# A slot directive at the head of TensorE's HGRN loop

## The chip, the cores and the metric

The program runs on one core of a Trainium2 chip. The metric is the device time of one execution in microseconds (us), the median of several runs. Each engine of the core (TensorE, VectorE, ScalarE, GpSimd, SyncE) has its own instruction stream and its own sequencer, which reads that stream in order; the engines wait for each other on semaphores only. In the profile TensorE's matmuls are PE, its weight loads PEld, and what its sequencer handles by itself (register, semaphore and branch instructions) PEldq.

## What is computed

Two blocks of network layers over a sequence of 512 tokens and 16 meta tokens, width 1024, in float32. The stage that the change touches is the second layer of the first block, a gated linear recurrence (HGRN2):

```python
def hgrn2_mixer(h, w_in, lb, o_norm, w_out):
    q, fp, i_in, gate = jnp.split(h @ w_in, 4, axis=-1)
    q = jax.nn.silu(q)
    f = lb32 + (1.0 - lb32) * jax.nn.sigmoid(fp32)
    k = (1.0 - lb32) * jax.nn.sigmoid(-fp32)
    ...
    _, o = lax.scan(_hgrn_chunk_step, S0, xs)   # S_t = diag(f_t) S_{t-1} + k_t i_t^T, o_t = S_t^T q_t
    ...
    return (o * jax.nn.silu(gate)) @ w_out
```

There are 16 heads of 128 channels. Ahead of this stage comes a pooling layer, behind it two layers of windowed attention with a gated MLP. All large products are made in three parts: each float32 operand is split into a high and a low part, and high by high, low by high and high by low are accumulated.

## The kernel before

The engines' programs are written out by hand; the order of TensorE's work is the order of the Python code, unrolled, save for one loop. `products` (L402 to L404) issues the three matmuls of one 128x128 tile of weights; `unit` runs it over a whole projection of 128 output channels (24 matmuls of 512 columns, or 48 of 264). Each matmul is two instructions in TensorE's stream, a weight load and the matmul.

The HGRN stage works on pairs of heads, eight in all. `b_pair` (from L1235) makes the eight projections of one pair of heads and, in between, at the places in `STEP_AT`, the steps of the recurrence of the pair before (`b_tensor_step`, from L564). These steps are short matmuls. The recurrence is solved level by level: `first_products` (L541) and `level_products` (L552 and L560), with 128 columns by 32 rows of weights and 16 columns of data. Steps 2 and 3 of each pair are bursts of 128 such matmuls at L560, 256 instructions each; each step begins with waits that are register and semaphore instructions (L568, L574 to L577). Each pair so has an L541 burst of 64 matmuls, two L560 bursts of 128 and one L552 burst of 64.

The pairs are placed as follows: one `b_pair` without a recurrence; then the loop (L1263), run twice, each time with two pairs (`"odd"`, `"even"`) and an output projection `b_out`; then three more `b_pair` calls, the last pair's steps, and all later layers, unrolled. The loop's body is 3,320 instructions in TensorE's stream: 1,588 weight loads, 1,588 matmuls and 144 register, semaphore and branch instructions. Ahead of its first instruction stand the two waits of L1261 and L1262 and the register move that sets the loop's counter; behind it 13,035 instructions follow. The loop ends in an addition and a compare-and-branch, both attributed to L1263. The other engines have loops of their own, which the change doesn't touch. SyncE issues the loads of weights, 1 MB each, as TensorE's finished units free their buffers.

Of the kernel before, what the change touches and what calls it, by code (L numbers as in the profile page):

```python
# [137 lines left out]
def program(nc, a, out):  # L138
    with ExitStack() as ctx:
# [752 lines left out]
        def _(sp):  # L892
# [47 lines left out]
            def load_pair(i, part):  # L940
                pair, _, before = pair_units(i, part)
                for n, col in enumerate((E, 0, 2 * E, 3 * E)):
                    load_chunk(sp, n, n % 2, w_in_b[:, :, bass.ds(col + 256 * pair, 256)], "k8",
                               before + 2 * n - 2 + CREDIT)
# [129 lines left out]
        def _(pe):  # L1074
# [157 lines left out]
            def b_pair(i, part, process):  # L1232

                pair, u0, p0 = pair_units(i, part)
                slot = 0  # L1235

                def side():
                    nonlocal slot
                    if process is not None and slot in STEP_AT:
                        b_tensor_step(pe, STEP_AT[slot], *process)  # L1240
                    slot += 1

                for j, (what, x) in enumerate(PAIR_UNITS):
                    pe.wait_ge(acc_done[x], pair_half(part, i) + j // 2)
                    pe.wait_ge(lo_ready, p0 + j + 1 + CREDIT)
                    first = part == "first" and j == 0
                    unit(pe, x, "k8", j, 0, KT, of_x, T if what in "fi" else SEQ,
                         (lambda k: pe.wait_ge(xlo_ready, KT + k + 1)) if first else None, side,
                         mean_squares if first else None)
                    side()  # L1250

            def b_out(g, u0h, p0):
                z = lambda k, t0, w: (zhib[:, k, :], zlob[:, k, :])
                for n in range(OUT_UNITS):
                    pe.wait_ge(acc_done[n % 2], u0h + n // 2)
                    pe.wait_ge(lo_ready, p0 + n // 2 + 1 + CREDIT)
                    unit(pe, n % 2, "k4", n // 2, n % 2, GT, z, SEQ,
                         (lambda k: pe.wait_ge(zblo_ready, 4 * g + k + 1)) if n == 0 else None)

            b_pair(None, "first", None)  # L1260
            pe.wait_ge(a_zero, 2)  # L1261
            pe.wait_ge(m_zero, 4)  # L1262
            with pe.Fori(0, NG - 2) as i:  # L1263
                b_pair(i, "odd", (2 * i, 0))
                b_pair(i, "even", (2 * i + 1, 1))
                b_out(i, UB // 2 + 12 + (B_STEPS // 2) * i, PB + 24 + B_PIECES * i)
# [1365 lines left out]
```

## Time and profile before

| | |
|---|---|
| median of 3 runs | 1562.62 us (1562.44 to 1562.76) |
| the profiled execution | 1562.62 us, of it 1560.8 us span from the first to the last instruction |
| PE busy | 1548.8 us, 99% of the span |
| weight loads, VectorE, ScalarE, GpSimd busy | 1390.4, 997.0, 603.0, 352.7 us |
| granted TensorE clock, mean | 0.999 of full speed |
| chain of work that ended last | 98% PE |
| transfers of instructions, queue q8 | 103 packets, 1.69 MB |

The 1.8 us between the execution's time and its span lie before the first and behind the last instruction. The page divides the span by engine and line; its chain follows the work back from the last instruction. "issue" in it is time in which the engine waited for nothing that the profile shows.

### The profile page before, as it was taken

How to read it: one execution, taken by the hardware profiler on the slowest of the kernel's cores; microseconds unless marked ns; L12 is line 12 of the kernel's file. 1: busy time of each engine (PE TensorE's matmuls, PEld its weight loads, DVE VectorE, ACT ScalarE, POOL GpSimd, SP SyncE). 2: the span in 40 equal slices, each digit the busy share in tenths (PEclk: the TensorE clock that was granted, in tenths of full speed). 3: DMA queues.
4: the chain of work that ended last, by engine and by line, in shares of the span. 5: the costliest groups of instructions: out<-in, count | busy, mean ns of one | idle time of the engine just before them, and what ended most of it. 6: DMA issues, size and time to landing. Idle time of an engine off the chain costs nothing.

```text
span 1560.8 us, 30500 instructions
## 1 busy us (share of the span) xinstructions
PE 1548.8 (99%) x12567; PEld 1390.4 (89%) x12567; DVE 997.0 (64%) x1622; ACT 603.0 (39%) x1102; POOL 352.7 (23%) x333
## 2 busy tenths in 40 slices
PE   9999999999999999999999999999999999999998
PEld 9999999999899899899898898888888988888887
DVE  6665565764767568576786677567615785676346
ACT  5323122253454344434445445573113247541121
POOL 0000000020321124031231224334430043343510
PEclk9999999999999999999999999999999999999999
DMA  5323223223121322221222132222233332222331
GB/s 169 109 81 105 86 82 92 99 81 114 56 81 56 92 73 83 82 83 55 83 83 95 56 124 92 81 82 81 85 105 135 112 99 82 82 81 81 110 133 54
DMA packets 113721, 141.08 MB, mean 90 GB/s; under 512 B 3020, under 2 KB 90480, under 8 KB 113584
## 3 DMA queue, kind: packets, MB, share of 16 engines
q1 hardware_dynamic: 109872, 134.38, 26.9%
q10 hardware_dynamic: 3632, 4.53, 0.9%
q8 instruction: 103, 1.69, 0.4%
q14 instruction: 34, 0.28, 0.1%
q0 software_dynamic: 80, 0.20, 0.0%
HBM read 137.01 MB, written 2.10 MB: 89 GB/s over the span
## 4 chain that ended last, share of the span: by engine, by line
PE 98%; DVE 1%; issue 0%; DMA 0%; SPq 0%; ACT 0%; ACTq 0%
PE acc L402 28%; PE acc L404 28%; PE acc L403 28%; PE aux L560 1%; PE aux L402 1%; PE aux L404 1%; PE aux L403 1%; PE aux L628 1%; PE aux L630 1%; PE aux L1358 1%; PE aux L1388 1%; PE aux L620 1%; PE aux L541 1%; PE aux L1377 1%; PE aux L1378 0%; PE aux L1412 0%
## 5 line engine op out<-in xcount | busy, mean ns | idle before, releaser
L402 PE MATMUL acc<-xhis,whi 128*128 128x264 f32 (+2 forms) x1848 | 611.9, 331 | 0.0
L404 PE MATMUL acc<-xhis,wlo 128*128 128x264 f32 (+2 forms) x1848 | 602.2, 326 | 0.0
L403 PE MATMUL acc<-xlos,whi 128*128 128x264 f32 (+2 forms) x1848 | 601.8, 326 | 0.0
L402 PEld LDWEIGHTS acc<-xhis,whi 128*128 128x128 f32 x1848 | 348.0, 188 | 29.2 <-issue 0.5
L404 PEld LDWEIGHTS acc<-xhis,wlo 128*128 128x128 f32 x1848 | 347.9, 188 | 29.3
L403 PEld LDWEIGHTS acc<-xlos,whi 128*128 128x128 f32 x1848 | 348.3, 188 | 26.8
L397 POOL TENSOR_TENSOR wlo<-raw,whi 128x1024 fp32r<-128x1024 f32 x84 | 207.7, 2473 | 377.0 <-DVE whi L2489 377.0
L393 ACT ACTIVATE whi<-raw 128x1024 fp32r<-128x1024 f32 x158 | 164.1, 1048 | 131.7 <-PE acc L404 118.7
L397 DVE TENSOR_TENSOR wlo<-raw,whi 128x1024 fp32r<-128x1024 f32 x81 | 99.8, 1236 | 36.9 <-ACT whi L393 36.7
L2186 DVE TENSOR_TENSOR wlo<-raw,whi 128x1024 fp32r<-128x1024 f32 x77 | 93.8, 1220 | 22.4 <-ACT whi L393 22.2
L2489 DVE CAST whi<-raw 128x1024 fp32r<-128x1024 f32 x84 | 66.8, 797 | 54.0 <-PE acc L404 53.8
L1050 POOL TENSOR_TENSOR kb<-kb,fb 128x264 f32<-128x264 f32 x16 | 16.2, 1032 | 293.4 <-PE aux L541 293.4
L1020 POOL TENSOR_TENSOR xns<-sqs 128x528 f32<-128x528 f32 x1 | 1.5, 1462 | 323.8 <-ACT sqs L1646 323.8
L402 PE MATMUL acc<-zhia,whi 128*128 128x264 f32 x256 | 73.3, 286 | 0.0
L404 PE MATMUL acc<-zhia,wlo 128*128 128x264 f32 x256 | 72.9, 285 | 0.0
L403 PE MATMUL acc<-zloa,whi 128*128 128x264 f32 x256 | 72.7, 284 | 0.0
L402 PEld LDWEIGHTS acc<-zhia,whi 128*128 128x128 f32 x256 | 48.1, 188 | 0.2
L404 PEld LDWEIGHTS acc<-zhia,wlo 128*128 128x128 f32 x256 | 48.2, 188 | 0.0
L403 PEld LDWEIGHTS acc<-zloa,whi 128*128 128x128 f32 x256 | 48.2, 188 | 0.0
L2101 DVE TENSOR_TENSOR h<-acc,h 128x528 f32<-128x528 f32 x32 | 22.6, 707 | 38.9 <-PE acc L404 38.9
L1804 ACT ACTIVATE pr<-sc,sm 128x257 f32<-128x257 f32 (+1 forms) x64 | 30.4, 478 | 19.7 <-DVE sm L2421 19.6
L772 ACT ACTIVATE sqs<-aux 128x128 f32<-128x128 f32 x56 | 14.7, 277 | 57.3 <-PE aux L630 57.3
(394 smaller groups left out, 2824.4 us busy)
## 6 DMA issues: line engine op xcount, KB each, us to landing
raw<-in_w_in SPq DMA_DIRECT2D x38, 1024.0 KB, 5.2
raw<-in_hgrn_w_in SPq DMA_DIRECT2D x32, 1024.0 KB, 5.7
raw<-in_pool_w_in SPq DMA_DIRECT2D x15, 1024.0 KB, 5.5
raw<-in_pool_w_out SPq DMA_DIRECT2D x8, 1024.0 KB, 5.1
raw<-in_hgrn_w_out SPq DMA_DIRECT2D x8, 1024.0 KB, 5.1
raw<-in_w_out SPq DMA_DIRECT2D x8, 1024.0 KB, 5.1
raw<-in_pool_w_grp SPq DMA_DIRECT2D x4, 1024.0 KB, 5.1
raw<-in_w_branch_attn SPq DMA_DIRECT2D x4, 1024.0 KB, 5.1
```

What stands on the lines that cost most here:

```text
L393: act.activation(piece(whi, kind, m), raw_view(kind, m), ACT.Copy).then_inc(hi_ready, 1)
L397: dve.tensor_tensor(piece(wlo, kind, m), raw_view(kind, m), piece(whi, kind, m), ALU.subtract).then_inc(lo_ready, 1)
L402: pe.matmul(dst, stat[0], mov[0], start=first, stop=False)
L403: pe.matmul(dst, stat[0], mov[1], start=False, stop=False)
L404: return pe.matmul(dst, stat[1], mov[0], start=False, stop=last)
L541: mm = pe.matmul(first_bank(c, x)[rows, :, col:col + 32], kb[par][x][:, META + t0:META + t0 + 32], both[:, :, t0:t0 + 32], start=True, sto ...
L560: mm = pe.matmul(dst.rearrange("p (b m) -> p b m", m=m), keys, second_halves(mov, m), start=True, stop=True)
L1050: pool.tensor_tensor(first_halves(dst, m), first_halves(src, m), both[:, :, 1].unsqueeze(2).to_broadcast([P, both.shape[1], m]), ALU.mult)\
L1804: act.activation(pr[z][:, x, lo:], sc[z][:, x, lo:], ACT.Exp, bias=sm[z][:, 0, x:x + 1], accum_out=sm[z][:, 1, x:x + 1])\
L2101: dve.tensor_tensor(halves(h[:, n, :]), acc_all(slot), halves(h[:, n, :]), ALU.add)\
L2186: dve.tensor_tensor(piece(wlo, kind, m), raw_view(kind, m), piece(whi, kind, m), ALU.subtract).then_inc(lo_ready, 1)
L2489: dve.tensor_copy(piece(whi, kind, M), raw_view(kind, M)).then_inc(hi_ready, 1)
```

## The change

TensorE's program gets one directive between the last wait and the loop:

```diff
             b_pair(None, "first", None)
             pe.wait_ge(a_zero, 2)
             pe.wait_ge(m_zero, 4)
+            pe.addr_align(256, offset=215)
             with pe.Fori(0, NG - 2) as i:
                 b_pair(i, "odd", (2 * i, 0))
```

## Rows read from the trace of the kernel before

**Rows 1.** The page: busy time of TensorE, engines on the chain, instruction queue.
```profile
PE 1548.8 (99%) x12567; PEld 1390.4 (89%) x12567; DVE 997.0 (64%) x1622; ACT 603.0 (39%) x1102; POOL 352.7 (23%) x333
...
q8 instruction: 103, 1.69, 0.4%
...
PE 98%; DVE 1%; issue 0%; DMA 0%; SPq 0%; ACT 0%; ACTq 0%
```

**Rows 2.** The chain in order of time, first and second round: start us, us, what.
```profile
402.89 1.21 PE aux L560 x83
404.10 1.18 issue
...
413.90 1.23 PE aux L560 x84
...
544.20 1.47 issue
```

**Rows 3.** Timeline of PE: start us, us, engine, line; two bursts and what follows.
```profile
402.82 0.45 PE L560 MATMUL aux<-q_first,kb 128*32 128x16 f32 x32
...
405.44 0.50 PE L402 MATMUL acc<-xhis,whi 128*128 128x512 f32 x1
...
462.67 0.45 PE L560 MATMUL aux<-q_first,kb 128*32 128x16 f32 x32
...
463.89 0.50 PE L402 MATMUL acc<-xhis,whi 128*128 128x512 f32 x1
```

**Rows 4.** DMA from 402.5 to 404.5 (40 slices of 0.05), then 542.9 to 544.3.
```profile
GB/s 0 0 0 0 0 0 0 0 328 0 0 0 0 0 0 0 0 0 0 0 0 0 0 0 0 0 0 0 0 0 0 0 0 0 0 0 0 0 20 123
...
q8 instruction: 1, 0.02, 2.9%
...
GB/s 0 0 0 468 0 0 0 0 0 0 0 0 0 0 0 0 0 0 0 0 0 0 0 0 0 0 0 0 0 0 0 0 0 0 0 0 0 0 0 0
```

**Rows 5.** Line L574 from 401.4 to 402.5: durations in ns, first and last start.
```profile
L574 PEldq ALU_OP  x1: 32/32/32, 401.5 to 401.5; - x1
```

**Rows 6.** Lines L1263 and L1262, the loop's own instructions and the wait before.
```profile
L1263 PEldq COMPARE_BRANCH  x2: 83/1830/3577, 522.2 to 662.6; - x2
L1263 PEldq MOVE  x1: 29/29/29, 382.1 to 382.1; - x1
...
L1262 PEldq EVENT_SEMAPHORE  x1: 51/51/51, 382.0 to 382.0; - x1
```

**Rows 7.** Timeline of PE where the loop begins for the first time.
```profile
385.85 0.39 PE L404 MATMUL acc<-xhis,wlo 128*128 128x512 f32 x1
386.07 0.28 PE L402 MATMUL acc<-xhis,whi 128*128 128x264 f32 x1
```

**Rows 8.** DMA from 522 to 526, in 40 slices of 0.1 us.
```profile
GB/s 0 0 0 0 0 0 0 0 0 0 0 164 0 0 0 0 0 0 0 0 0 0 0 0 20 92 195 225 266 215 225 246 215 164 225 174 195 195 195 236
```

**Rows 9.** Timeline of TensorE behind the loop's branch back.
```profile
525.91 0.39 PE L404 MATMUL acc<-zhib,wlo 128*128 128x512 f32 x1
526.08 0.19 PEld L402 LDWEIGHTS acc<-xhis,whi 128*128 128x128 f32 x1 [0.20 <-issue]
...
528.37 0.28 PE L402 MATMUL acc<-xhis,whi 128*128 128x264 f32 x1
```

**Rows 10.** DMA from 524 to 529 (slices of 0.125 us), then 528.1 to 529.3 (0.03 us).
```profile
DMA  0000357977797876898789899999999999412000
...
GB/s 273 273 307 785 273 239 171 103 103 103 34 34 34 34 307 0 34 34 0 34 0 0 0 0 0 0 0 0 0 0 0 0 0 0 0 0 0 0 0 0
```

**Rows 11.** Lines L568 and L577 from 409 to 411, ends of ten successive instructions.
```profile
L568 PEldq ALU_OP  x2: 32/32/32, 409.7 to 410.2; - x2
...
L577 PEldq ALU_OP  x2: 32/32/32, 410.1 to 410.5; - x2
```

**Rows 12.** DMA from 414 to 420 (slices of 0.15 us), and PE near its end.
```profile
DMA  0000001665658699968999999999978792000000
...
419.77 0.28 PE L404 MATMUL acc<-xhis,wlo 128*128 128x264 f32 x1
```

## The prediction, made before the changed kernel ran

> **What bounds the kernel now.** I read the page first. PE is busy for 99% of the span and makes up 98% of the chain [rows 1], so time that TensorE's matmuls gain or lose at one place moves the end by as much; no other engine can hide it, and none is close to taking over. Then I asked what is left between the matmuls. The chain in order of time has only two pauses of over a microsecond within TensorE's stream that no other engine explains, 1.18 and 1.47 us, both marked "issue", both inside the same L560 burst (steps of the first pair of the body), once in each of the two rounds of the loop [rows 2]. Burst and successor take 2.62 us there (402.82 to 405.44); the same burst of the second pair takes 1.22 us (462.67 to 463.89) [rows 3]. The first pause so costs 1.40 us and the second, 0.29 us longer, 1.69 us: 3.09 us in all.
>
> The instruction queue tells what they are. It moved 1.69 MB in 103 packets [rows 1], 16.4 KB each; at 64 bytes a slot that is 256 slots, and the 25,893 instructions that TensorE executes are 101 such blocks. One block starts to move at 402.9, the other time at 543.0, just as the burst starts, and nothing else moves then [rows 4]. The sequencer is seen at L574 at 401.5, three instructions before the burst [rows 5], and the first late instruction follows at 405.28, 2.4 us after the packet's start and 3.8 us after L574. So a block is fetched when the sequencer enters the one before it, takes about 3.7 us to be usable, and a burst of 256 instructions that runs off in 1.2 us gets to its end first. The branch back gives the same price without a burst: it takes 3.577 us [rows 6], with a packet at 523.1 [rows 8].
>
> **Where the blocks lie.** The late instruction is the 643rd of the body: I count 308 weight loads, 308 matmuls and 26 register and semaphore instructions ahead of it. If it opens a block, the loop's first instruction now stands 642 - 2x256 = 130 slots before a block's end, that is in slot 126, and the move before it in slot 124 or 125. The burst begins 390 slots into the body, at slot 126 + 390 = 516, slot 4 of its block: nearly the whole burst lies in one block, entered just ahead of it. The second pair's burst lies 1,555 slots on, slot 23, and has no pause.
>
> **What the change does to the two pauses.** The move goes to slot 215, so all boundaries lie 90 or 91 slots earlier in the code. The burst then begins at slot 94, and 162 of its 256 instructions lie ahead of the next boundary. The block that it needs in its middle was asked for 94 slots earlier, some 6 us. Both pauses go: **-3.09 us** [rows 2, 3]. I went through the twelve L560 bursts of the six placements (in the loop two pairs, behind it four) with their distances. First bursts begin at slots 94, 113, 75, 66, 57 and 215, second bursts at 177, 196, 153, 144, 135 and 28. None lies within some ten slots of a block's start as the slow one does. The nearest cases are those with one boundary inside a burst and the next a little behind it; a dozen or more long matmuls lie between entry and need there, at 0.12 us each or more [rows 12, 9], and only one of them is tight enough to be a rival, below. A block of long matmuls alone lasts 15 us.
>
> **What the padding costs.** 90 or 91 empty instructions are executed once. The matmuls still queued cover part of it: the sequencer is through with the wait of L1262 at 382.0 and with the move at 382.1 [rows 6], but the loop's first matmul starts at 386.07, the last one before it at 385.85 [rows 7]. The queue so holds 3.7 us, from which the move and two register instructions take 0.3: **3.4 us are hidden**. That is 0.038 us for each of 90. The trace of before has no empty instruction of TensorE. From below the bound is nothing: 256 weight loads and matmuls pass in 1.22 us [rows 3], under 0.005 us each. From above: ten successive register and semaphore instructions start between 409.7 and 410.5 [rows 11], 0.093 us each; a wait takes 0.051 of its own instead of 0.032 [rows 6, 11], so some 0.11. Without the 0.032 that are the register instruction's own, 0.061 are left: an instruction without work lies between 0.061 and 0.093. I take the middle, 0.077: 90 x 0.077 = 6.9, less 3.4, **+3.5 us** (range 0 to +6.5). It is nearest to the register rows, since both are handled by the sequencer, not by the array.
> [...]
>
> **What the branch back costs.** Now the branch finds TensorE with 3.6 us of queued matmuls, which run out as it ends: the next weight load starts at 526.08 after 0.20 us of idle [rows 9]. Behind it stand 130 slots of the head's block. After the change only 40 slots stand there: two register instructions and 19 matmuls; the 20th, which starts at 528.37 [rows 9], is in the next block. In the trace of before that next block's packet starts at 528.2, at the end of a 1 MB load of weights that runs from 524.5 to 528.7 [rows 10]. With 2.4 us from packet to use, as at 402.9, it is there at 530.6. Before, 90 slots more lay between, and the trace shows no pause there. After the change PE stands from 528.37 to 530.6: **+2.2 us**, once, as there is one branch back. If the load didn't hold it up, 525.8 + 3.6 = 529.4 and +1.0 us are the lower value; nothing, if the next block comes along with the head's. I take 2.2, since the load stands in the same place by TensorE's clock of events.
>
> **Sum.** -3.09 + 3.5 + 2.2 = +2.6 us on the profiled execution's 1562.62 us, which is the median too: **1565.2 us**.
>
> **The rivals.** (a) Padding at the full price of a register instruction or a wait, 0.093 to 0.11 us: 8.4 to 9.9 us, 5.0 to 6.5 visible, total +4.1 to +5.6, so 1566.7 to 1568.2. For it speaks that no instruction of TensorE's sequencer in the trace is seen closer to the next than these [rows 11]; against it that an empty one reads and writes no register. This is the one that ends on the slower side; it decides from 0.083 us per slot on, where the sum passes +3.1.
> (b) Padding passes as fast as matmuls do, under 0.038 us, and is hidden: -3.09 + 2.2 = -0.9, 1561.7. (c) Padding as in my sum, but the next block is there after the branch: +0.4, 1563.0. (d) Both are free: -3.09, 1559.5; this is the most that can be gained. (e) A further pause: the block entered at 414.0, early in the second burst of the first pair [rows 2], is followed, with the new boundaries, by one needed at 419.77, while a load of weights fills the engines from 415.0 to 419.2 [rows 12]. A packet held until the load's end, 418.8, would be usable at 421.2: 1.4 us in each round, 1568.0. Against it: the request goes out 1.0 us ahead of the load, and the packet of 402.9 started 1.4 us behind L574 [rows 4, 5], so that this one would be only just inside the load.
> (f) The pauses aren't fetches, and stay. The trace ties each to a packet and finds both in one slot of the code, so this has little for it: +3.5 for the padding, and 1566.1. [...]
>
> **How the numbers follow.** My case (padding between 0.061 and 0.092, back edge at 1.5 to 2.7) gets 0.38, of which some 0.12 lie above +3.1; (a) 0.24; (b) 0.15; (c) 0.08; (d) 0.05; (e) 0.07; (f) 0.03. A kernel as steady as this one can be told from no change at about 0.2%, that is 3.1 us: below 1559.5 faster, above 1565.7 slower. Faster is (d) at its edge, 0.05. Slower is (a), (e), (f) and the upper part of mine: 0.24 + 0.07 + 0.03 + 0.12 = 0.46. Within: 0.49. The range reaches from (b) with a little of its back edge off, 1561.0, to (e) and the top of (a), 1568.0. The likeliest case alone spans 1563.6 to 1566.9.
>
> **What would show it.** In the trace of after: no "issue" in the L560 bursts near 403 and 543; the first L541 burst later by the visible part of the padding, with PE idle before the loop's first matmul (3.5 us is my number; none would mean (b)); behind the branch back PE idle after 19 matmuls of 264 columns, for some 2 us; nothing new near 419.8 or 560; the queue's packets 90 slots earlier in the code. I am wrong if the pauses move with the padding instead of going, if the padding is seen nowhere, or if an idle stretch of several microseconds ahead of the loop makes the granted clock fall, of which the pauses of up to 1.47 us in this trace give no sign.

## The result and the profile after

The changed kernel takes 1565.69 us, the median of 10 runs (1564.4 to 1571.59), the kernel before 1562.53 (10 runs, 1561.85 to 1563.07). The ratio is 1.0025 with a 95% interval of 1.0017 to 1.0032: **slower by 0.25%**. That it is slower at all is clear. Whether it is slower by more than the 0.2% that the prediction set as its bound is not: 0.2% lies within the interval, and the median lies on the bound that the prediction gave in microseconds, 1565.7. The profiled execution took 1564.61 us, of it 1562.8 us span, 2.0 us more than the one of before.

The page of after. TensorE works as before; the matmuls that wait for nothing the profile shows are the news:

```profile
PE 1548.5 (99%) x12567; PEld 1390.5 (89%) x12567; DVE 997.1 (64%) x1622; ACT 603.8 (39%) x1102; POOL 354.6 (23%) x333
...
L402 PE MATMUL acc<-xhis,whi 128*128 128x264 f32 (+2 forms) x1848 | 611.8, 331 | 2.8 <-issue 2.8
L403 PE MATMUL acc<-xlos,whi 128*128 128x264 f32 (+2 forms) x1848 | 601.9, 326 | 1.9 <-issue 1.9
```

The busy time is that of [rows 1] within 0.3 us, so all of the difference is idle time. It lies at two places. TensorE's timeline of after at the loop's first matmul and, behind the branch back, at the 19th and 20th matmul of the second round:

```profile
385.89 0.39 PE L404 MATMUL acc<-xhis,wlo 128*128 128x512 f32 x1
389.03 0.39 PE L402 MATMUL acc<-xhis,whi 128*128 128x264 f32 x1 [2.75 <-issue]
...
529.93 0.28 PE L402 MATMUL acc<-xhis,whi 128*128 128x264 f32 x1
532.15 0.39 PE L403 MATMUL acc<-xlos,whi 128*128 128x264 f32 x1 [1.93 <-issue]
```

In [rows 7] the loop's first matmul came at 386.07 behind one at 385.85. What filled the first gap is on record too. The loop's lines in the trace of after (the directive has line L1263 now, the loop L1264):

```profile
L1263 PEldq NOP  x90: 13/13/13, 382.2 to 388.7; - x90
...
L1264 PEldq COMPARE_BRANCH  x2: 83/1728/3372, 523.8 to 664.6; - x2
L1264 PEldq MOVE  x1: 29/29/29, 388.7 to 388.7; - x1
```

Ninety empty instructions, 13 ns long each but 0.073 us apart (6.5 us for 89 steps), end where the move begins. They are all that the directive's line has in this trace; with the offset at 165, 50 less, there are 40 (e10_slot165). The branch back takes 3.372 us instead of the 3.577 of [rows 6]. And the bursts: where [rows 2] had pauses of 1.18 and 1.47 us, the chain in order of time of after has none, in either round.

```profile
405.96 1.23 PE aux L560 x84
407.18 0.43 PE acc L402
```

```profile
546.77 1.22 PE aux L560 x85
547.99 0.43 PE acc L402
```

I followed the start of each matmul in both traces and took after minus before. The difference grows by 3.0 us at the loop's entry, shrinks by 1.4 at the first burst, grows by 2.2 behind the branch back and shrinks by 1.7 at the second burst. That makes 2.1 us, and it ends at 2.0.

One thing isn't in this trace. It shows the clock at full speed behind the idle ahead of the loop (us; busy times of PE, PEld, DVE, ACT, POOL; granted clock; DMA):

```profile
389.00:400.00 11.00, 10.97 (x146) 10.76 (x146) 3.54 (x6) 3.51 (x7) 0.20 (x1) 1.00 0.07 23
```

But of the ten runs of the changed kernel, five have a mean granted clock of 0.999 and take 1564.4 to 1565.34 us, median 1564.6, the time of the profiled one. The others have 0.998 to 0.995 and take 1566.05, 1566.05, 1566.95, 1569.37 and 1571.59 us, with lower clocks in the longer ones (0.995 in the last two).

### The profile page after: what moved, and what is told of

Read it like the earlier page. It is cut to its first block, busy times and chain, and to the rows that moved or that the text cites. A ratio compares the mean times of both kernels' runs of the same rounds, so it can differ in the third digit from the quotient of the medians.

```text
span 1562.8 us, 30590 instructions
## 1 busy us (share of the span) xinstructions
PE 1548.5 (99%) x12567; PEld 1390.5 (89%) x12567; DVE 997.1 (64%) x1622; ACT 603.8 (39%) x1102; POOL 354.6 (23%) x333
## 3 DMA queue, kind: packets, MB, share of 16 engines
q8 instruction: 103, 1.69, 0.5%
## 4 chain that ended last, share of the span: by engine, by line
PE 98%; DVE 1%; issue 0%; DMA 0%; SPq 0%
PE acc L402 28%; PE acc L404 28%; PE acc L403 28%; PE aux L560 1%; PE aux L402 1%; PE aux L404 1%; PE aux L403 1%; PE aux L628 1%; PE aux L630 1%; PE aux L1359 1%; PE aux L1389 1%; PE aux L620 1%; PE aux L541 1%; PE aux L1378 1%; PE aux L1379 0%
```

## The experiments

In all of them the code of `b_pair` and everything else is that of the kernel before unless told; they differ in the lines ahead of the loop. With `max_nops=0` the padding is branched over: for the 90 empty instructions the directive's line has one and a compare-and-branch of 185 ns (e1_branch215; 317 ns in e2_slot91), and the move starts 0.4 us behind the empty one (382.7 to 383.1; 0.6 us in e2_slot91) instead of 6.5 us.

### The slots without the padding

```diff
             pe.wait_ge(m_zero, 4)
+            pe.addr_align(256, offset=215, max_nops=0)
             with pe.Fori(0, NG - 2) as i:
```

> The same slots as after the change, with the padding branched over instead of executed. Theory (three independent terms: the two L560 pauses, the executed padding, the branch back): the 2.75 us of idle ahead of the loop go, the 1.93 us behind the branch back stay, no pause in the L560 bursts; 1562.6 - 3.09 + 2.0 + 0.1 for one branch = 1561.6 us. Rival (the move of the code as such costs, the padding is only beside it): it stays at 1564.6 or above. On the runs of the changed kernel with a mean granted clock of 0.995 to 0.998: if the idle of 2.75 us ahead of the loop lets the clock fall, all runs are at 0.999 here; if the 1.93 us do it, some are still below.

Measured: 1562.69 us (11 runs, 1562.02 to 1563.74), ratio 1.0002 (0.9993 to 1.0011). Who waited for whom on PE: the 2.8 is gone, the other has stayed.

```profile
PE acc L403 <- issue: 2.1, 1, 2.1
```

There is no pause in any L560 burst. So the executed padding is a cost by itself: the loop's entry costs 3.0 us in the changed kernel and nothing here, and the two execute from the same slots. (That their medians are 3.0 us apart as well is a coincidence: the median of the changed kernel has its runs of lower clock in it, and this kernel loses the 0.6 us told below.) The time came out 1.1 us above what was expected. Some of that is the branch back: matmul by matmul it costs 2.4 us here, against 2.2 after the change. The stage as a whole gains 1.4, loses 2.4 and gains 1.7 us, together a gain of 0.7. But 0.6 us more than before is lost in the first 10 us of the program, where TensorE waits for the first data, so that this trace ends level with that of before. That loss is in this trace and in some of the others but not in that of the changed kernel; whether it stands for more than single executions is open.

The clock's part of the expectation is met in part. None of the eleven runs has a mean clock below 0.998, and none is above 1563.74. But not all are at 0.999, as expected if only the 2.75 us let the clock fall: seven are (1562.02 to 1562.93), and four are at 0.998 (1563.09 to 1563.74). A mean of 0.998 alone says little. The single run of e5_branch195 has it too, and in its trace the clock is at 0.50 only at the program's end, where no matmul is left:

```profile
10.00:1551.70 1541.70, 1540.08 (x12517) 1383.06 (x12516) 989.95 (x1608) 599.07 (x1094) 355.28 (x323) 1.00 0.28 89
...
1554.20:1558.90 4.70, 0.00 (x0) 0.00 (x0) 2.21 (x4) 0.00 (x0) 0.00 (x0) 0.50 0.29 112
```

Why the four are also the four longest, by 0.8 us in the median, stays open. The profiled run is not one of them.

### Slots at which nothing is left

```diff
+            pe.addr_align(256, offset=91, max_nops=0)
```

> The loop's first instruction in slot 92, padding branched over: 164 slots stand behind the branch back's target in its block, and the first pair's L560 burst begins in slot 226. Theory: neither pause, nor padding, nor idle of more than 0.3 us behind the branch back: 1562.6 - 3.09 + 0.1 = 1559.6 us. Rival (a load of weights or another burst takes the place of what was removed): 1561 us or more, with a new pause in one of the later L560 bursts, of which the closest to a block's start are in slots 245, 11 and 20.

Measured: **1559.89 us** (11 runs, 1559.37 to 1560.56), ratio 0.9982 (0.9973 to 0.9991). The list of PE's waits has no "issue" row at all. All runs are at a clock of 0.999. This is the best version found: 2.8 us ahead of the kernel before and 5.8 ahead of the change, from the place of the code alone.

### The padding without the slots

```diff
+            pe.addr_align(256, offset=215)
+            pe.addr_align(256, offset=125, max_nops=0)
```

> The 90 padding instructions of the change executed, and then a branch on to the slots of the kernel before, so that no boundary moves. Theory: idle of 2.8 to 3.0 us ahead of the loop, both L560 pauses of 1.2 and 1.5 us as before, 0.2 us of idle behind the branch back: 1562.6 + 3.1 = 1565.7 us. Rival (fetches depend on time, not on the slots): the pauses change or go. If the idle ahead of the loop is what lets the clock fall, some of these runs show a mean clock of 0.998 or less and are 1 to 7 us above the rest.

Measured: 1567.67 us (7 runs, 1565.36 to 1569.0), ratio 1.0031 (1.002 to 1.0043). Chain in order of time, at the loop's entry, in the first and in the second round:

```profile
386.13 3.11 issue
...
407.70 1.21 PE aux L560 x83
408.91 1.33 issue
```

```profile
548.27 1.21 PE aux L560 x83
549.48 1.19 issue
```

The pauses come behind the same 83 of the burst's records as in [rows 2]: they belong to slots, not to a moment. Their lengths differ from those of [rows 2] by 0.15 and 0.28 us, so a single pause is known no better than that. The second thing that this trace shows is why some runs are longer than the sum. The timeline behind the idle, and the granted clock in three stretches (columns as in the rows of the clock above):

```profile
389.23 0.38 PE L402 MATMUL acc<-xhis,whi 128*128 128x264 f32 x1 [3.11 <-issue]
389.45 0.29 PE L403 MATMUL acc<-xlos,whi 128*128 128x264 f32 x1
...
391.76 0.42 PE L403 MATMUL acc<-xlos,whi 128*128 128x264 f32 x1
391.98 0.42 PE L404 MATMUL acc<-xhis,wlo 128*128 128x264 f32 x1
```

```profile
389.20:391.00 1.80, 1.77 (x10) 1.77 (x11) 1.80 (x4) 0.00 (x0) 0.00 (x0) 0.69 0.12 38
391.00:393.00 2.00, 2.00 (x11) 2.00 (x10) 0.53 (x1) 0.00 (x0) 0.00 (x0) 0.50 0.00 0
393.00:396.00 3.00, 3.00 (x27) 2.96 (x26) 0.00 (x0) 1.38 (x4) 0.00 (x0) 0.95 0.00 0
```

After 3.11 us without a matmul the granted clock is 0.69 and then 0.50 of full speed, and the matmuls of 264 columns are 0.22 us apart instead of 0.12 until 393.1. Matmul by matmul that costs 1.5 us on top of the idle. Of the seven runs, two take 1565.36 and 1565.45 us, with a mean clock of 0.998 and 0.999: that is the time that was expected without a fall of the clock. The other five, the profiled one among them, take 1567.07 to 1569.0 us at 0.996 to 0.998.

### Fewer slots behind the branch's target

```diff
+            pe.addr_align(256, offset=235, max_nops=0)
```

> The loop's first instruction in slot 236, padding branched over: only 20 slots, 2 register instructions and 9 matmuls, stand behind the branch back's target in its block, 10 matmuls of 0.12 us fewer than after the change. Theory (the next block is asked for when the branch lands, and its arrival doesn't depend on the slot): PE idles after 9 matmuls, for 1.93 + 1.2 = 3.1 us; the time is 1562.6 - 3.09 + 3.3 = 1562.8 us. Rival (the next block is asked for only when the sequencer gets to it): it is asked for earlier too, and the idle stays near 1.9 us, 1561.6 us.

Measured, one run: 1564.7 us. The idle comes after exactly nine matmuls:

```profile
525.86 0.28 PE L403 MATMUL acc<-xlos,whi 128*128 128x264 f32 x1
525.98 0.28 PE L404 MATMUL acc<-xhis,wlo 128*128 128x264 f32 x1
529.49 0.39 PE L402 MATMUL acc<-xhis,whi 128*128 128x264 f32 x1 [3.22 <-issue]
```

3.1 was expected and 3.22 measured; the rival's 1.9 is out. The time is 1.9 us above what was expected, because the clock falls here too, behind this idle instead of the loop's entry. It costs 1.6 us:

```profile
531.00:533.00 2.00, 2.00 (x11) 2.00 (x11) 0.00 (x0) 0.00 (x0) 0.00 (x0) 0.50 0.00 0
```

### More slots behind the branch's target

```diff
+            pe.addr_align(256, offset=195, max_nops=0)
```

> The loop's first instruction in slot 196, padding branched over: 60 slots, 2 register instructions and 29 matmuls, behind the branch back's target in its block. Theory (arrival fixed, matmuls hide it at 0.12 us each): idle of 2.14 - 10 x 0.12 = 0.9 us after 29 matmuls, and the clock stays. Rival (the idle depends on the block boundary alone): about 2 us again.

Measured, one run: 1560.7 us, idle of 0.98 us where 0.9 was expected, in front of the L604 product in which slot 256 falls (28 matmuls, not the 29 of the expectation: two register and semaphore instructions stand among them).

```profile
529.28 0.28 PE L604 MATMUL aux<-ident,ib 128*16 128x128 f32 x1 [0.98 <-issue]
```

With 20, 40 and 60 slots the idle is 3.2, 2.1 and 1.0 us: ten matmuls, 1.2 us by their own pace, are worth 1.1 us.

### What holds that block up

The load of weights was the sum's explanation for the 2.2 us. To test it, the load was made small.

```diff
-            sp.dma_start(raw[slot][:, :].rearrange("p (k n) -> p k n", n=w), src)\
+            sp.dma_start(raw[slot][:, :].rearrange("p (k n) -> p k n", n=w)[:, 0:rows, :], src[:, 0:rows, :])\
...
-                               before + 2 * n - 2 + CREDIT)
+                               before + 2 * n - 2 + CREDIT, 1 if part == "odd" and n < 2 else None)
```

> As e1_branch215, but the first two loads of weights of each odd pair, in the loop and once behind it, bring only the first 128 KB of their 1 MB; the projections made from the rest use what the buffer held, so this leaves out part of the data's movement and computes other values. Theory (the load in flight holds up the block behind the branch back): its packet starts 1.0 to 1.4 us after the branch has landed instead of 2.5, and PE's idle behind the 19 matmuls shrinks from 2.1 us to 0.9 +- 0.3. Rival (2.5 us is what it takes after a taken branch, load or not): packet and idle stay as they were.

Measured, one run: 1561.8 us, idle of 1.86 us. This one tells nothing: the loads that I had shrunk were over by then. The DMA queues of this kernel from 522 to 531 still have the whole megabyte.

```profile
q1 hardware_dynamic: 1040, 1.05, 38.9%
q8 instruction: 2, 0.03, 1.3%
```

The next kernel has `n == 2` in the place of `n < 2`, which is the load in flight.

> As e8_small_load, which shrank two other loads: here the third load of each odd pair, the one in flight when the branch lands, brings 128 KB of its 1 MB, and the rest of its projections is computed from what the buffer held. Theory (the load holds up the block behind the branch's target): the block's packet starts 1.0 to 1.4 us after the branch has landed instead of 2.3 to 2.5, and PE's idle is 0.9 +- 0.3 us instead of 1.9 to 2.1. Rival (2.4 us is what it takes after a taken branch): both stay.

Measured, one run: 1560.54 us.

```profile
527.63 0.28 PE L402 MATMUL acc<-xhis,whi 128*128 128x264 f32 x1
528.13 0.39 PE L403 MATMUL acc<-xlos,whi 128*128 128x264 f32 x1 [0.22 <-issue]
```

The DMA's rate from 522 to 530 in slices of 0.2 us, this kernel and e1_branch215, whose branches both land at 525.1:

```profile
GB/s 0 82 0 0 0 0 0 0 82 200 277 97 0 0 0 0 0 0 82 0 0 0 0 0 0 0 0 0 41 0 0 0 0 0 0 0 0 82 0 0
```

```profile
GB/s 0 82 0 0 0 0 0 0 26 210 215 179 261 241 169 169 205 230 251 236 307 364 384 379 394 353 328 343 97 20 5 0 0 0 0 0 0 0 0 0
```

Without the load the next block's packet stands alone in the 19th slice, 0.7 us behind the landing; with it, the packet lies within the load, at 527.4, 2.3 us behind. The idle shrinks from 2.14 to 0.22 us. So the rival is out, on one run: 1.9 of the 2.1 us are contention with the load, and even the lower value of the prediction, 1.0, was too high for a free DMA.

### How close a burst may come

```diff
+            pe.addr_align(256, offset=130, max_nops=0)
```

> The loop's first instruction in slot 131, five later than before: the first pair's L560 burst begins in slot 9 instead of 4, so its block is entered at the register instruction that is done at 400.6 instead of 401.5. Theory (block usable 3.7 us after entry): the two pauses shrink by about 0.9 us, to some 0.4 to 0.6 us of idle each; time 1562.6 - 2.0 = 1560.6 us. Rival (a burst that nearly fills a block pauses as long wherever it begins): 1.2 and 1.5 us as before.

Measured, one run: 1560.3 us, and **no pause** at all, where 0.4 to 0.6 us were expected.

```profile
403.51 1.23 PE aux L560 x85
404.74 0.43 PE acc L402
```

The expectation took the block's entry from the end of the wait at L574. The rate from 400 to 404, in slices of 0.1 us, has the packet at 400.9:

```profile
GB/s 0 0 0 0 0 0 0 0 0 164 0 0 0 0 0 0 0 0 0 0 0 0 0 0 0 0 0 0 0 0 0 0 0 0 0 0 0 0 0 0
```

That is 2.5 us ahead of the burst; in the kernel before it was 0.1 us behind its first matmul [rows 3, 4]. In the kernel before, the burst's block begins with the second L574 of the two groups of waits, at 401.5 [rows 5]. Here, five slots later, it begins with the first L574:

```profile
L574 PEldq FUSED_REGOPS  x1: 37/37/37, 401.2 to 401.2; - x1
```

This record stands 1.3 us behind the one ahead of it, L568 at 399.9, and 0.3 us behind the packet. So the request was out before L574 was through: while the sequencer stood at that wait, it had entered the new block. Five slots take the whole pause away.

```diff
+            pe.addr_align(256, offset=117, max_nops=0)
```

> The loop's first instruction in slot 118: the first pair's L560 burst begins in slot 252, 4 slots ahead of a boundary, and the next boundary lies 4 slots behind its end. Theory: the block is entered at 401.9 by the clock of before, usable at 405.6, needed 2 matmuls of 512 columns behind the burst, at 404.6: idle of 0.9 to 1.2 us there instead of inside the burst, in both rounds; time 1562.6 - 0.8 = 1561.8 us. Rival (only a boundary inside a burst can stall it): no pause, 1559.6 us.

Measured, one run: 1561.95 us. The pause has left the burst and stands two matmuls behind it, 0.71 us in the first round and 0.91 in the second.

```profile
404.33 0.50 PE L402 MATMUL acc<-xhis,whi 128*128 128x512 f32 x1
404.67 0.40 PE L403 MATMUL acc<-xlos,whi 128*128 128x512 f32 x1
405.77 0.50 PE L404 MATMUL acc<-xhis,wlo 128*128 128x512 f32 x1 [0.71 <-issue]
```

1.10 us from matmul to matmul instead of 0.23: 0.9 us lost. So a boundary needn't lie in the burst; it is the time between two boundaries that counts.

### A padding that is hidden

```diff
+            pe.addr_align(256, offset=165)
```

> The directive as in the change, padding executed, but slot 165: 40 empty instructions, 90 slots behind the branch's target in its block, the first pair's L560 burst in slot 44. Theory: 40 x 0.073 = 2.9 us of padding are under the 3.4 us of queued matmuls, so no idle ahead of the loop beyond 0.2 us; 44 matmuls cover the block behind the branch; no pause, clock at 0.999 in all runs: 1562.6 - 3.09 = 1559.6 us, the time of e2_slot91. Rival (any executed padding costs its full time): 1562.5 us.

Measured: 1560.89 us (11 runs, 1559.81 to 1561.57), ratio 0.999 (0.9981 to 0.9999). The padding is there, and costs nothing: the loop's first matmul follows in step.

```profile
L1263 PEldq NOP  x40: 13/13/13, 382.9 to 385.7; - x40
```

```profile
386.63 0.39 PE L404 MATMUL acc<-xhis,wlo 128*128 128x512 f32 x1
386.86 0.28 PE L402 MATMUL acc<-xhis,whi 128*128 128x264 f32 x1
```

But the time is 1.3 us above the expected one. The chain in order of time says where:

```profile
797.73 1.19 PE aux L560 x83
798.92 1.18 issue
```

It is the first L560 burst of the third pair behind the loop.

```profile
800.11 0.24 PE L560 MATMUL aux<-q_second,xns 128*32 128x16 f32 x3 [1.18 <-issue]
```

At slot 215 it began in slot 57 by the prediction's list, so with the code 50 slots earlier it begins in slot 7. (By the trace it is slot 5 or 6: three matmuls come late here, where two did at slot 4, at 405.28 in the trace of before. The list is off by one or two there.) I had checked the pairs in the loop alone. The same pause at a third place, in a slot between 4, where it is whole, and 9, where it is gone, speaks for the mechanism more than a hit would have.

## Why the prediction was right, and where it wasn't

**The two pauses** (-3.09 us). They were fetches of instruction blocks, as said: gone after the change, -1.4 and -1.7 us, back in e3_padding_only at unchanged slots, and in e10_slot165 at another pair that came to lie as the first one had. In the trace of before the queue moved 103 blocks [rows 1], and PE's waits on "issue" are these two alone (2.6 us together); rival (f) falls. One detail was wrong: the prediction dated the entry into a block by the end of the wait at L574, and e6_slot130 shows the request out before that. The prediction took 64 bytes a slot and 256 slots a block as given. Measured are 1.69 MB in 103 packets [rows 1] for TensorE's 25,893 instructions, 65 bytes for one and 251 of them to a packet; and 40, 20 and 60 instructions of the loop ahead of the idle behind the branch back with the loop's first one at slot 216, 236 and 196 by the directive (the changed kernel, e4_branch235, e5_branch195), 256 in sum each time.

**The padding** (+3.5 us, at 0.077 us each). The price was a guess between two register rows and is 0.073 us. The trace has the empty instructions as the sequencer's (PEldq), like the registers'. The cover by queued matmuls was put at 3.4 us: 90 x 0.073 = 6.6, less 3.4, is 3.2, and 3.0 is what the entry lost. Forty of them vanish wholly. Rivals (a) and (b) fall.

**The branch back** (+2.2 us). Right in place, after 19 matmuls, and in size, 2.2. Right also in its cause, with one correction: the lower bound of 1.0 rested on 3.6 us from landing to use with a free DMA, and in e9_third_load it is 3.0 us (525.1 to 528.13), with 0.2 us of idle. The packet starts 0.7 us after the landing there.

**The sum.** Predicted +2.6 to 1565.2 us. The profiled execution has +2.0; the median of all runs, 1565.69, has +3.2. The first difference is the padding's price and its cover, 0.5 us. The second is a term that the sum didn't have: I named a fall of the clock as what would prove me wrong, gave it no price, and took from pauses of up to 1.47 us that there would be none. Half of the runs are longer by it, as far as is known. The two differences have opposite signs, so that the sum comes within 0.5 us of the median is in part luck. In the runs at a clock of 0.999 the change costs 2.1 us, which is within 0.2%. With the others the median comes to lie on the bound between "within", which had 0.49, and "slower", which had 0.46 from cases that didn't come true; the runs don't settle which side it is on, and what brought it there is outside the sum. That the clock falls after 3.1 and 3.2 us of idle is shown by two traces. That the same happened in the longer runs of the changed kernel, behind its 2.75 us, is argued and not shown. For it speak their mean clock and e1_branch215, which lacks that idle and has no run below 0.998. But no trace caught it: the one trace of the changed kernel has the 2.75 us and no fall. And a low mean comes without that idle too: of the 15 runs of the kernel before that were taken beside e10_slot165, one is at 0.997 and is the longest, 1563.61 us.

**The rest.** Rival (e), a pause near 419.8, didn't come. My list of bursts held in all traces where I used it, and cost me a miss where I didn't. What stays open is why the first 10 us differ by up to 0.8 us between single executions, and how the two slowest runs of the changed kernel came to a mean clock of 0.995. One fall, as in e3_padding_only, leaves the mean at 0.998. As an estimate from these means, 0.995 takes three or four such falls; at 1.5 us each they are 4.5 to 6 us, near the 4.8 and 7.0 us that the two runs are longer than the median of those at 0.999. Where in the program they would lie, nothing here shows.

## What to carry to other kernels

Where one engine's stream is the critical path, a pause marked "issue" at the same instruction in each round is to be held against the instruction queue's packets: where the sequencer crosses a block faster than the next one comes (here a burst of 256 instructions in 1.22 us, against 3.8 us from L574 to the late instruction), or lands a branch near a block's end while a large load is in flight (here 40 slots ahead of it, 2.2 us), the place of the code is worth microseconds: 1559.89 us in e2_slot91, 1562.53 before. Moving it moves every boundary behind it too, so all short, dense bursts have to be listed for the new place (1.18 us of pause in e10_slot165 at one that wasn't), and padding is free only as long as queued work lasts (40 empty instructions cost nothing here, 90 cost 3.0 us). An idle stretch of the array of 3.1 or 3.2 us cost half as much again in granted clock here (1.5 and 1.6 us).

## What the runs showed of the hardware

- An empty instruction on TensorE's sequencer is 13 ns long on record and takes 0.073 us of its time (90 from 382.2 to 388.7 after the change), while the short weight loads and matmuls of a burst passed in under 0.005 us each (256 in 1.22 us, [rows 3]).
- Behind the branch back the next block's packet started 0.7 us after the landing with a free DMA (e9_third_load, PE idle for 0.22 us), 2.3 us after it with a 1 MB load in flight (e1_branch215, 2.14 us).
- In e6_slot130 the request for the next block was out before a wait in the new block was over: the packet stands at 400.9 and the block's first instruction, a wait's, at 401.2. The pauses of 1.18 and 1.47 us [rows 2] are gone there.
- After 3.11 and 3.22 us without a matmul the granted clock was 0.50 for a stretch, which cost 1.5 and 1.6 us; the traces with 2.75, 2.14 and 1.93 us of idle show no such stretch.
